# Mixture of experts, scatter back to the tokens: four experts' slot rows of one tile of tokens in 128 rows instead of two experts' rows of both tiles

## Chip, cores and metric

One core of one Trainium2 chip. The metric is the device time of one execution in microseconds (us), lower is better; the figure for a kernel is the median of its timed runs.

## What is computed

A trunk of two layers over 256 tokens (two tiles of 128) of width 1024. Each layer has a mixer of four head groups, a cross-attention into 256 memory tokens, and a grouped mixture of experts, each followed by a layer norm. The change touches the mixture of experts alone:

```python
# grouped_moe, cut
for e in range(N_EXPERTS):                                   # 16 experts
    h = jax.nn.silu(xt @ w_gate[e]) * (xt @ w_up[e])         # 1024 -> 256
    out = out + gates[:, e:e + 1] * (h @ w_down[e])          # 256 -> 1024
# gates: two experts per token, both inside the best of four groups; all others are 0
x = layer_norm(ALPHA * x + out, ln3_g[l], ln3_b[l])
```

## The kernel before, in words

Every token goes to two of the 16 experts, so the kernel doesn't multiply all tokens with all experts. It gives each expert 64 **slots**: 32 for tokens of tile 0 and 32 for tokens of tile 1 (a dense branch stands by for inputs that don't fit). The expert weights, 48 matrices of 1 MB per layer, stream from HBM through a ring of 12 buffers (`RING`, in the order of `expert_units`: gate and up matrices of pair j, then the down matrices of pair j-1). The sync engine's queue issues the loads in that order (`load`, L493; the DMA is issued on L512), and each waits until PE has finished with the matrix that lay in the buffer before.

The stage, per layer:

- DVE builds **one-hots** from each token's place (`one_hot`, L1531, the operation on L1534): per tile of tokens and half of the experts a 128x512 matrix, in which the columns of the other tile are zero. PE **gathers** token columns into slots with them (`part`, L2043, `gather_early`, `gather_late`), ACT and DVE move the result out of PSUM (`early_move`, `late_move`, L1572, L1580).
- PE brings each slot's gate value to its slot row (`gates_of_slots`, L2092, matmuls on L2096); DVE adds the high and low parts into `slot_gates` (L1612, L1617). PE transposes the one-hots (`to_token_turns`, L2100, transposes on L2105), ACT rounds the result into `to_token` (L967).
- For each **pair** j of experts (the two experts' 64 slots each fill 128 rows): `gate(j)`, `up(j)` (both L2122), the hidden values on ACT (`slots_tanh`, L923) and DVE (`hidden`, L1587, L1591), `turn(j)` (two transposes, L2144, moved by `turned_move`, L951), `down(j)` (16 matmuls in two halves of 512 columns, L2157).
- The output of `down(j)` is 128 slot rows by 1024 columns in PSUM. **Copies:** ACT rounds each half of 512 columns to `y_hi` (`out_high`, L953, operation on L958), DVE subtracts and leaves the rest in `y_lo` (`out_low`, L1594, operation on L1597). Two 128x512 operations on each engine per pair.
- **Scatter:** `scatter(j)` (L2163, matmuls on L2169) adds the pair's rows to the tokens' sum in the PSUM tensor `quad`: for each tile of tokens and each half of the columns one matmul with `y_hi` and one with `y_lo`, 8 matmuls of 512 columns a pair. Half of the 128 rows that each of them contracts over belong to slots of the other tile and are zero in `to_token`.

PE's order is written out at the end of its layer loop: the loop `for j in range(2, PAIRS)` runs gate(j), up(j), scatter(j-2), turn(j), down(j-1), and down(7) and the scatters of pairs 6 and 7 follow. DVE runs `hidden(j)`, then `out_low(j-1)`, and after the last `out_low` the third norm (`third_norm`, L1163): it adds `quad` to `X` (L1077) for tile 0 once `quad_ready` is set, then for tile 1 once `moe_done` is set. DVE takes its instructions in order, so the norm stands behind all copies.

Of the kernel before, what the change touches and what calls it, by code (L numbers as in the profile page):

```python
# [101 lines left out]
def hybrid_trunk_kernel(nc, x, mem, positions, w_in, gmlp_v_norm_g, gmlp_w_s, gmlp_b_s, mla_q_norm_g,  # L102
# [16 lines left out]
    PAIRS = E // 2  # L119
    MOE = expert_units(E)  # L120
# [53 lines left out]
    with ExitStack() as ctx:  # L174
# [60 lines left out]
        half_gates = sb("half_gates", [P, T, PAIRS, 4], F32R)  # L235
        before = sb("before", [P, P])
        slots = sb("slots", [P, T, EXPERT_SLOTS])
# [80 lines left out]
        to_token = rounded("to_token", 6000, PAIRS, SEQ)  # L318
# [11 lines left out]
        def to_slot(t):  # L330

            return (y_hi, y_lo)[t][:, 4:8, :].rearrange("p a b -> p (a b)")
# [20 lines left out]
        def y_of(y, j, a):  # L353

            return y[:, 4 * (j % 2) + 2 * a:4 * (j % 2) + 2 * a + 2, :]

# [208 lines left out]
        def _(pool):  # L565
# [13 lines left out]
            for t in range(T):  # L579
                nc.gpsimd.iota(slots[:, t, :], pattern=[[1, EXPERT_SLOTS]], base=-P - TILE_SLOTS * t,  # L580
                               channel_multiplier=0, allow_small_or_imprecise_dtypes=True)
# [93 lines left out]
        def _(act):  # L675
# [85 lines left out]
            for l in range(DEPTH):  # L761
# [165 lines left out]
                with act.If(act.value_load(fits[0:1, 0:1], min_val=0, max_val=1)):  # L927
# [38 lines left out]
                    for b in range(4):  # L966
# [13 lines left out]
                with act.Else():  # L980
# [13 lines left out]
                    act.sem_inc(out_hi, 2 * PAIRS)  # L994
# [4 lines left out]
        def _(dve):  # L999
# [182 lines left out]
            for l in range(DEPTH):  # L1182
# [348 lines left out]
                def one_hot(half, t):  # L1531

                    mine = place[:, t, E // 2 * half:E // 2 * (half + 1)]
                    nc.vector.tensor_tensor(to_slot(t)[:, 512 * half:512 * half + 512].rearrange("p (e s) -> p e s", e=E // 2),  # L1534
                                            view(slots[:, t, :], [[0, E // 2], [1, EXPERT_SLOTS]]),
                                            view(mine, [[1, E // 2], [0, EXPERT_SLOTS]]), ALU.is_equal).then_inc(slots_ready, 1)

                def all_gates():
# [5 lines left out]
                    of_pairs = gates[:].rearrange("p t (j e) -> p (t j) e", e=2)  # L1544
                    halves = half_gates[:].rearrange("p t j e -> p (t j) e")
                    nc.vector.tensor_scalar(halves[:, :, 0:2], of_pairs, 0.5, None, ALU.mult)
                    dve.drain()
                    nc.vector.scalar_tensor_tensor(halves[:, :, 2:4], of_pairs, 0.5, halves[:, :, 0:2].bitcast(F32),
# [762 lines left out]
```

## Time and profile before

| | |
|---|---|
| median of 3 runs | 722.87 us (722.40 to 724.38) |
| the profiled execution, its own time | 723.68 us |
| span of the profiled execution | 721.8 us |
| PE (matmul) busy | 697.4 us, 97% of the span |
| DVE busy | 408.0 us, 57% |
| ACT busy | 280.5 us, 39% |
| moved by DMA | 176.10 MB |

The profile is one execution. Times inside it count from the start of the span. PE is the matmul engine, DVE the vector engine, ACT the scalar engine. A timeline row gives start, duration, engine, line, operation, output and inputs, shape and how many instructions were merged; the brackets at its end hold the idle time before it and what ended that. Rows of one engine that follow each other closely can overlap by the depth of its pipeline, so the distance from start to start is the cost of one in a row. The stage of the experts stands in the trace from about 242 to 357 us (layer 1) and from about 594 to 709 us (layer 2).

### The profile page before, as it was taken

To read this page: it belongs to the slowest core of one execution; us is meant where nothing else is said; L and a number is where in the kernel's file an instruction comes from. 1 tells how busy PE (TensorE), PEld (TensorE's weight loads), DVE (VectorE), ACT (ScalarE), POOL (GpSimd) and SP (SyncE) were. 2 spreads that over 40 slices of the span, in tenths; PEclk is the share of its full clock that TensorE was granted. 3 is DMA by queue.
4 is the path that set the end of the run, shared out by engine and by line. 5 is a ranking of instruction groups with operands and counts; after the bars stand their busy time and mean duration, and the time that the engine had idled before them with its cause. 6 is when DMAs were issued, how large, how long until landed. Compare 5 with 4: busy or idle time off the path is not lost.

```text
span 721.8 us, 11939 instructions
## 1 busy us (share of the span) xinstructions
PE 697.4 (97%) x4744; PEld 560.4 (78%) x4744; DVE 408.0 (57%) x724; ACT 280.5 (39%) x471; POOL 48.3 (7%) x93
## 2 busy tenths in 40 slices
PE   7999999999999999999799999999999999999992
PEld 7989987889988875656399798888898897655551
DVE  4885886674575752111477588848646567212126
ACT  3545643355543331111424466435455252311111
POOL 1720000010041000000011000001000010000000
PEclk9999999999999999999989999999999999999997
DMA  8991334574358499999985313445633685999961
GB/s 283 332 366 57 113 126 171 186 238 153 118 189 343 191 382 400 414 417 414 359 298 168 127 59 118 157 164 194 239 124 110 239 349 222 355 420 417 415 269 61
DMA packets 62702, 176.10 MB, mean 244 GB/s; under 512 B 3872, under 2 KB 37104, under 8 KB 53424
## 3 DMA queue, kind: packets, MB, share of 16 engines
q1 hardware_dynamic: 58112, 161.69, 60.2%
q0 software_dynamic: 4096, 12.25, 5.1%
q10 hardware_dynamic: 432, 1.31, 0.5%
q8 instruction: 41, 0.67, 0.4%
q14 instruction: 21, 0.17, 0.1%
HBM read 174.19 MB, written 1.05 MB: 243 GB/s over the span
## 4 chain that ended last, share of the span: by engine, by line
PE 60%; issue 31%; DVE 3%; POOL 2%; DMA 1%; ACT 1%; DVEq 1%; POOLq 0%; ACTq 0%
PE ring L2122 8%; PE ring L1688 7%; PE ring L1689 7%; PE ring L1690 7%; PE ring L2157 4%; PE quad L1688 4%; PE quad L1689 4%; PE quad L1690 4%; PE quad L2169 2%; PE ring L1730 2%; PE ring L1856 1%; PE ring L1759 1%; DMA X<-in_x 1%; PE ring L1749 1%; PE ring L1954 1%
## 5 line engine op out<-in xcount | busy, mean ns | idle before, releaser
L1004 DVE TENSOR_TENSOR w_lo<-raw,w_hi 128x1024 fp32r<-128x1024 f32 x108 | 127.7, 1222 | 39.0 <-ACT w_hi L691 33.9
L691 ACT CAST w_hi<-raw 128x1024 fp32r<-128x1024 f32 x108 | 108.0, 1049 | 65.1 <-PE quad L1690 60.3
L1688 PE MATMUL ring<-x_hi,w_hi 128*128 128x256 f32 x320 | 92.9, 290 | 0.8 <-ACTq L734 0.7
L1689 PE MATMUL ring<-x_lo,w_hi 128*128 128x256 f32 x320 | 90.5, 283 | 0.0
L1690 PE MATMUL ring<-x_hi,w_lo 128*128 128x256 f32 x320 | 90.5, 283 | 0.0
L714 ACT ACTIVATE arena<-ring 128x512 f32<-128x512 f32 (+1 forms) x66 | 35.5, 573 | 84.7 <-PE ring L1690 65.1
L1597 DVE TENSOR_TENSOR y_lo<-ring,y_hi 128x512 fp32r<-128x512 f32 x32 | 22.1, 692 | 72.9 <-ACT y_hi L958 72.9
L1688 PEld LDWEIGHTS ring<-x_hi,w_hi 128*128 128x128 f32 x320 | 61.3, 192 | 2.3 <-issue 1.9
L1689 PEld LDWEIGHTS ring<-x_lo,w_hi 128*128 128x128 f32 x320 | 61.3, 192 | 0.7 <-issue 0.5
L1690 PEld LDWEIGHTS ring<-x_hi,w_lo 128*128 128x128 f32 x320 | 61.3, 192 | 0.0
L2122 PE MATMUL ring<-raw,x_slots 128*64 128x256 f32 x448 | 51.3, 380 | 0.0
L1688 PE MATMUL quad<-w_hi,y_hi 128*128 128x512 f32 x128 | 51.1, 399 | 0.0
L1689 PE MATMUL quad<-w_lo,y_hi 128*128 128x512 f32 x128 | 50.0, 391 | 0.0
L1690 PE MATMUL quad<-w_hi,y_lo 128*128 128x512 f32 x128 | 49.9, 390 | 0.0
L2122 PEld LDWEIGHTS ring<-raw,x_slots 128*64 128x64 f32 x448 | 32.0, 137 | 16.9 <-issue 1.1
L2122 PE MATMUL ring<-w_raw,x_slots 128*64 128x256 f32 x160 | 36.9, 380 | 0.0
L1688 PE MATMUL ring<-xb_hi,w_hi 128*128 128x256 f32 x128 | 36.5, 285 | 0.0
L2157 PE MATMUL ring<-w_raw,arena 128*64 128x512 f32 x144 | 36.1, 598 | 0.0
L1689 PE MATMUL ring<-xb_lo,w_hi 128*128 128x256 f32 x128 | 35.7, 279 | 0.0
L1690 PE MATMUL ring<-xb_hi,w_lo 128*128 128x256 f32 x128 | 35.7, 279 | 0.0
L1730 PE MATMUL ring<-ident 128*128 128x128 f32 x204 | 28.2, 301 | 6.9 <-issue 4.0
L958 ACT CAST y_hi<-ring 128x512 fp32r<-128x512 f32 x32 | 18.8, 586 | 41.4 <-PE ring L2157 41.4
(322 smaller groups left out, 1421.5 us busy)
## 6 DMA issues: line engine op xcount, KB each, us to landing
raw<-in_moe_w_gate SPq DMA_DIRECT2D x20, 1024.0 KB, 7.0
w_raw<-in_moe_w_down SPq DMA_DIRECT2D x18, 1024.0 KB, 10.9
raw<-in_moe_w_up SPq DMA_DIRECT2D x16, 1024.0 KB, 7.7
raw<-in_w_in SPq DMA_DIRECT2D x14, 1024.0 KB, 11.3
raw<-in_moe_w_down SPq DMA_DIRECT2D x12, 1024.0 KB, 10.1
raw<-in_w_out SPq DMA_DIRECT2D x10, 1024.0 KB, 5.1
raw<-in_xattn_wk SPq DMA_DIRECT2D x8, 1024.0 KB, 5.9
raw<-in_xattn_wv SPq DMA_DIRECT2D x8, 1024.0 KB, 4.8
```

The source lines that it names most:

```text
L691: nc.scalar.copy(unit_slot(u, 0, n)[:, s], raw[:, SLOT[u], s]).then_inc(hi_done, 1)
L714: nc.scalar.activation(dst, src, ACT.Copy, scale=scale).then_inc(act_emptied, 1)
L958: nc.scalar.copy(y_of(y_hi, j, a), out_bank(j, a).rearrange("p (a b) -> p a b", a=2)).then_inc(out_hi, 1)
L1004: low = nc.vector.tensor_tensor(unit_slot(u, 1, n)[:, s], raw[:, SLOT[u], s], unit_slot(u, 0, n)[:, s].bitcast(F32), ALU.subtract)
L1597: last = nc.vector.tensor_tensor(y_of(y_lo, j, a), out_bank(j, a).rearrange("p (a b) -> p a b", a=2), y_of(y_hi, j, a).bitcast(F32), ALU.s ...
L1688: mm(out, a_hi, b_hi, start=first, stop=False)
L1689: mm(out, a_hi, b_lo, start=False, stop=False)
L1690: return mm(out, a_lo, b_hi, start=False, stop=last)
L1730: mm(o[:, 0:P], ident[:], ident[:], start=True, stop=True)
L2122: r = mm(ring[of_pair(i), b, 0:FF], rows_of(2 * j + i, c), w[i][:, c, :], start=c == 0, stop=c == DC - 1)
L2157: r = mm(out_bank(j, a)[of_pair(i), :], h_t[:, j % 2, c * P:(c + 1) * P][:, of_pair(i)], w[i][:, c, 512 * a:512 * a + 512], start=c == 0, ...
L2169: r = mm(quad[:, 2 * t + a, :], to_token[:, j, t * P:(t + 1) * P], y_of(y, j, a).rearrange("p a b -> p (a b)"), start=j == 0 and i == 0, s ...
```

## The change

The slots stay (64 per expert, 32 per tile), and so do `gate`, `up`, `turn` and the matmuls of `down`. What changes is how the output rows are laid out for the scatter.

- `y_hi` and `y_lo` hold the rows of **four** experts (two pairs) for one tile of tokens: 4 x 32 = 128 rows. Each half of a pair's output is copied in four **quarters** of 32 rows by 512 columns, which start at another row in the output than in the input (`quarters`). So ACT and DVE each issue 8 operations of 32x512 a pair instead of 2 of 128x512, each with its own semaphore step.
- `scatter(k)` runs once for four experts: 8 matmuls of 512 columns for two pairs instead of 16. In the loop over pairs it stands at the odd j alone; at the even j `turn(j)` stands between the two halves of `down(j-1)`. After `down(7)` 8 matmuls follow instead of 16.
- The one-hots lose their zero columns: 128x256 instead of 128x512. There are 8 transposes instead of 16, 8 matmuls of 8 columns for the gates instead of 16 of 4, two moves to `to_token` instead of four.
- `slot_gates` is made by 8 reductions over 32 rows instead of two copies and two additions over 64 rows.

```diff
+        def quarters(j):
+            for t in range(T):
+                for i in range(2):
+                    q = 2 * (j % 2) + i
+                    yield t, slice(32 * q, 32 * q + 32), slice(64 * i + 32 * t, 64 * i + 32 * t + 32)
...
@@ ACT, out_high(j) @@
-                            nc.scalar.copy(y_of(y_hi, j, a),
-                                           out_bank(j, a).rearrange("p (a b) -> p a b", a=2)).then_inc(out_hi, 1)
+                            for t, to, rows in quarters(j):
+                                nc.scalar.copy(y_of(y_hi, t, a)[to],
+                                               out_bank(j, a)[rows].rearrange("p (a b) -> p a b", a=2)).then_inc(out_hi, 1)
...
-                    for b in range(4):
+                    for b in range(2):
                         last = nc.scalar.copy(to_token[:, 2 * b:2 * b + 2, :],
...
@@ DVE, out_low(j) @@
-                            dve.wait_ge(out_hi, l * 2 * PAIRS + (2 * j + a + 1))
-                            last = nc.vector.tensor_tensor(y_of(y_lo, j, a),
...
+                            for n, (t, to, rows) in enumerate(quarters(j)):
+                                dve.wait_ge(out_hi, l * 8 * PAIRS + (8 * j + 4 * a + n + 1))
+                                nc.vector.tensor_tensor(y_of(y_lo, t, a)[to],
+                                                        out_bank(j, a)[rows].rearrange("p (a b) -> p a b", a=2),
+                                                        y_of(y_hi, t, a)[to].bitcast(F32), ALU.subtract).then_inc(out_split, 1)
...
@@ DVE, slot_gates @@
-                    for e in range(2):
-                        rows = of_pair(e)
-                        parts = ring[rows, 3, 0:2 * E].rearrange("p (j e) -> p e j", e=4)
-                        nc.vector.tensor_copy(slot_gates[rows, :], parts[:, e, :])
...
+                    for j in range(2):
+                        for t, q, rows in quarters(j):
+                            parts = ring[q, 3, 0:4 * E].rearrange("p (k t h e) -> p k t h e", k=FOURS, t=T, h=2)
+                            nc.vector.tensor_reduce(slot_gates[rows, :].rearrange("p (k j) -> p k j", j=2)[:, :, j],
+                                                    parts[:, :, t, :, q.start // 32], AX_X, ALU.add)
...
@@ PE, gates_of_slots; to_token_turns changes in the same way @@
-                        for j in range(PAIRS):
+                        for k in range(FOURS):
                             for t in range(T):
-                                r = mm(ring[:, 3, 4 * j:4 * j + 4], to_slot(t)[:, j * P:(j + 1) * P],
-                                       half_gates[:, t, j, :], start=t == 0, stop=t == T - 1)
+                                at_col = 8 * (2 * k + t)
+                                r = mm(ring[:, 3, at_col:at_col + 8], to_slot(t)[:, k * P:(k + 1) * P], half_gates[:, t, k, :],
+                                       start=True, stop=True)
...
@@ PE, down(j, halves=range(2)): waits for out_split of the pair before, as it did @@
+                            if 0 < j < PAIRS - 1:
+                                pe.wait_ge(out_split, l * 8 * PAIRS + 8 * j)
...
-                    def scatter(j, tiles=range(T)):
+                    def scatter(k, tiles=range(T)):
 
                         for t in tiles:
                             for a in range(2):
-                                pe.wait_ge(out_split, l * 2 * PAIRS + (2 * j + a + 1))
+                                pe.wait_ge(out_split, l * 8 * PAIRS + (8 * (2 * k + 1) + 4 * a + 2 * (t + 1)))
                                 for i, y in enumerate((y_hi, y_lo)):
-                                    r = mm(quad[:, 2 * t + a, :], to_token[:, j, t * P:(t + 1) * P],
...
+                                    r = mm(quad[:, 2 * t + a, :], to_token[:, k, t * P:(t + 1) * P],
...
@@ PE, the order @@
                     for j in range(2, PAIRS):
                         gate(j)
                         up(j)
-                        scatter(j - 2)
-                        turn(j)
-                        down(j - 1)
+                        if j % 2:
+                            scatter(j // 2 - 1)
+                            turn(j)
+                            down(j - 1)
+                        else:
+                            down(j - 1, (0,))
+                            turn(j)
+                            down(j - 1, (1,))
                     down(PAIRS - 1)
-                    scatter(PAIRS - 2, (0,))
-                    scatter(PAIRS - 1, (0,)).then_inc(quad_ready, 1)
-                    scatter(PAIRS - 2, (1,))
-                    scatter(PAIRS - 1, (1,)).then_inc(moe_done, 1)
+                    scatter(FOURS - 1, (0,)).then_inc(quad_ready, 1)
+                    scatter(FOURS - 1, (1,)).then_inc(moe_done, 1)
```

## Rows read from the trace of the kernel before

**Rows 1.** The page: busy time of the engines, then data moved in 40 equal slices.
```profile
PE 697.4 (97%) x4744; PEld 560.4 (78%) x4744; DVE 408.0 (57%) x724; ACT 280.5 (39%) x471; POOL 48.3 (7%) x93
...
GB/s 283 332 366 57 113 126 171 186 238 153 118 189 343 191 382 400 414 417 414 359 298 168 127 59 118 157 164 194 239 124 110 239 349 222 355 420 417 415 269 61
```

**Rows 2.** Timeline of PE, one period of the pair loop, layer 1.
```profile
269.09 3.65 PE L2157 MATMUL ring<-w_raw,arena 128*64 128x512 f32 x16
...
276.03 3.62 PE L2122 MATMUL ring<-raw,x_slots 128*64 128x256 f32 x32
279.58 0.51 PE L2169 MATMUL quad<-y_hi,to_token 128*128 128x512 f32 x1
...
281.55 0.38 PE L2144 MATMUL ring<-ident,arena 128*128 128x128 f32 x2
281.86 3.65 PE L2157 MATMUL ring<-raw,arena 128*64 128x512 f32 x16
```

**Rows 3.** PE at the stage's head: a wait (us, times, longest us), then its timeline.
```profile
PEld ring L2045 <- DVE xn_lo L1455: 0.7, 2, 0.3
...
253.53 0.27 PE L2096 MATMUL ring<-half_gates,y_hi 128*128 128x4 f32 x1
...
255.34 0.37 PE L2045 MATMUL quad<-y_hi,xn_hi 128*128 128x256 f32 x1
...
261.03 0.33 PE L2105 MATMUL quad<-ident,y_hi 128*128 128x128 f32 x1
...
262.84 0.38 PE L2144 MATMUL ring<-ident,arena 128*128 128x128 f32 x2
```

**Rows 4.** Stretches: five engines, PE clock, DMA busy share, GB/s.
```profile
250.00:276.00 26.00, 26.00 (x214) 17.98 (x212) 13.12 (x21) 7.68 (x14) 0.00 (x0) 1.00 0.89 347
276.00:347.00 71.00, 71.00 (x500) 41.13 (x498) 12.32 (x22) 10.41 (x22) 0.00 (x0) 1.00 1.02 415
```

**Rows 5.** Two loads alone: duration ns, issue time, then time from issue to landing.
```profile
L512 SPq DMA_DIRECT2D w_raw<-in_moe_w_up x1: 367/367/367, 318.5 to 318.5; - x1
...
DMA to landing us min/median/max: 18.5/18.5/18.5
...
L512 SPq DMA_DIRECT2D arena<-in_moe_w_down x1: 414/414/414, 327.9 to 327.9; - x1
...
DMA to landing us min/median/max: 19.3/19.3/19.3
```

**Rows 6.** Timeline of PE, first use of those two loads, and down(6).
```profile
339.89 0.38 PE L2122 MATMUL ring<-mem_kT,arena 128*64 128x256 f32 x1
...
345.73 4.08 PE L2157 MATMUL ring<-w_raw,arena 128*64 128x512 f32 x17
349.22 0.59 PE L2157 MATMUL ring<-arena 128*64 128x512 f32 x1
```

**Rows 7.** Timeline of ACT and DVE: copies of pairs 6 and 7, then the third norm.
```profile
347.71 0.59 ACT L958 CAST y_hi<-ring 128x512 fp32r<-128x512 f32 x1 [1.50 <-PE ring L2157]
...
348.33 0.69 DVE L1597 TENSOR_TENSOR y_lo<-ring,y_hi 128x512 fp32r<-128x512 f32 x1 [4.22 <-ACT y_hi L958]
...
353.48 0.69 DVE L1597 TENSOR_TENSOR y_lo<-ring,y_hi 128x512 fp32r<-128x512 f32 x1 [1.03 <-ACT y_hi L958]
355.00 1.28 DVE L1077 SCALAR_TENSOR_TENSOR X<-X,quad 128x512 f32<-128x512 f32 x2 [0.83 <-PE quad L2169]
```

**Rows 8.** Timeline of DVE: operations that follow each other without a gap.
```profile
366.03 1.29 DVE L1029 TENSOR_TENSOR x_lo<-ring,x_hi 128x512 fp32r<-128x512 f32 x2
...
380.73 0.42 DVE L1232 COPY arena<-ring 128x256 f32<-128x256 f32 x1 [1.83 <-PE ring L1690]
381.17 0.42 DVE L1235 TENSOR_TENSOR arena<-ring,rope_cos 32x256 f32<-32x256 f32 x1
381.61 0.43 DVE L1236 TENSOR_TENSOR arena<-ring,rope_sin 32x256 f32<-32x256 f32 x1
...
256.63 0.34 DVE L1612 COPY slot_gates<-ring 64x8 f32<-64x8 f32 x2 [0.21 <-issue]
```

More of the change, by code:

```diff
@@ L119, in hybrid_trunk_kernel @@
     PAIRS = E // 2
+    FOURS = E // 4
     MOE = expert_units(E)
@@ L234, in hybrid_trunk_kernel @@
         gates = sb("gates", [P, T, E])
-        half_gates = sb("half_gates", [P, T, PAIRS, 4], F32R)
+        half_gates = sb("half_gates", [P, T, FOURS, 8], F32R)
         before = sb("before", [P, P])
-        slots = sb("slots", [P, T, EXPERT_SLOTS])
+        slots = sb("slots", [P, TILE_SLOTS])
         place = sb("place", [P, T, E])
@@ L317, in hybrid_trunk_kernel @@
         h_t = at(4608, 2, FF)
-        to_token = rounded("to_token", 6000, PAIRS, SEQ)
+        to_token = rounded("to_token", 6000, FOURS, SEQ)
         x_third = at(8048, DC, SEQ)
@@ L578, in _ @@
                                     pattern=[[1, P]], channel_multiplier=-1)
-            for t in range(T):
-                nc.gpsimd.iota(slots[:, t, :], pattern=[[1, EXPERT_SLOTS]], base=-P - TILE_SLOTS * t,
-                               channel_multiplier=0, allow_small_or_imprecise_dtypes=True)
+            nc.gpsimd.iota(slots[:], pattern=[[1, TILE_SLOTS]], base=-P, channel_multiplier=0,
+                           allow_small_or_imprecise_dtypes=True)
             pool.drain().then_inc(ident_ready, 1)
@@ L1608, in _ @@
                     dve.wait_ge(slot_gated, l + 1)
-                    for e in range(2):
-                        rows = of_pair(e)
-                        parts = ring[rows, 3, 0:2 * E].rearrange("p (j e) -> p e j", e=4)
-                        nc.vector.tensor_copy(slot_gates[rows, :], parts[:, e, :])
-                    dve.drain()
-                    for e in range(2):
-                        rows = of_pair(e)
-                        parts = ring[rows, 3, 0:2 * E].rearrange("p (j e) -> p e j", e=4)
-                        nc.vector.tensor_tensor(slot_gates[rows, :], parts[:, 2 + e, :], slot_gates[rows, :], ALU.add)
+                    for j in range(2):
[3 more added lines that the diff above has]
+                                                    parts[:, :, t, :, q.start // 32], AX_X, ALU.add)
                     dve.drain()
@@ L2043, in part @@
                 def part(half, c, t, x_part, first=False, last=False):
-                    one_hot = to_slot(t)[:, 512 * half:512 * half + 512]
-                    return mm(tile_slots(gather_bank(half, c), t), x_part[:, t, c, :], tile_slots(one_hot, t), start=first,
-                              stop=last)
+                    one_hot = to_slot(t)[:, SEQ * half:SEQ * half + SEQ].rearrange("p (e s) -> p e s", e=E // 2)
+                    return mm(tile_slots(gather_bank(half, c), t), x_part[:, t, c, :], one_hot, start=first, stop=last)
                 def gather_early():
@@ L2145, in turn, with down @@
                         r.then_inc(turned, 1)
-                    def down(j):
-                        pe.wait_ge(turned_moved, l * PAIRS + (j + 1))
-                        if 0 < j < PAIRS - 1:
-                            pe.wait_ge(out_split, l * 2 * PAIRS + 2 * j)
+                    def down(j, halves=range(2)):
+                        if 0 in halves:
+                            pe.wait_ge(turned_moved, l * PAIRS + (j + 1))
+                            if 0 < j < PAIRS - 1:
+                                pe.wait_ge(out_split, l * 8 * PAIRS + 8 * j)
                         w = [v.rearrange("p (c n) -> p c n", c=2)
                              for v in pair_wait((down_unit(2 * j), down_unit(2 * j + 1)))]
-                        for a in range(2):
+                        for a in halves:
                             for c in range(2):
```

39 lines of the change are left out of this document (17 added, 22 removed).

## Prediction

> **What bounds the kernel now.** I read the page first: PE is busy for 697.4 of 721.8 us, and in two stretches of the kernel the data moved stand at 414 to 420 GB/s for several slices in a row [rows 1]. Both are the stage of the experts. Two limits are near each other there, so I then read PE's timeline, the loads one by one, and the end of the stage.
>
> PE's timeline shows no gap in the pair loop. One period, from down to down, is 281.86 - 269.09 = 12.77 us; the scatter takes 281.55 - 279.58 = 1.97 us of it, and gate or up without one behind it is 3.45 us long, with one 3.55 us (from 276.03 to 279.58) [rows 2].
>
> The loads tell the other half. A period uses 6 matrices of 1.049 MB, which is 6.29 MB in 12.77 us or 493 GB/s. The transfers give 415 GB/s from 276 to 347 us with a busy share of 1.02, after 347 GB/s and 0.89 from 250 to 276 us [rows 4]. So PE eats faster than the transfers deliver, and lives on the 12 matrices that lay ready. The reserve is almost gone at the end: the second up matrix of pair 7 lands at 318.5 + 18.5 = 337.0 us, the last down matrix at 327.9 + 19.3 = 347.2 us [rows 5], and PE starts on them at 339.89 and 349.22 us [rows 6]. The slack is 2.9 and 2.0 us.
>
> The third thing to see is what ends the stage. down(6) starts at 345.73 [rows 6], the first copy on ACT 1.98 us later, DVE's first subtraction 2.60 us later (348.33), the last one at 353.48, and the norm's addition for tile 0 at 355.00 us [rows 7]. I measure the stage by that 355.00, since everything behind it keeps its order.
>
> **The change part by part** (layer 1; layer 2 repeats it, so all is doubled at the end).
>
> *Head.* 16 gate matmuls take 255.34 - 253.53 = 1.81 us, 16 transposes 262.84 - 261.03 = 1.81 us [rows 3]. Half of each goes: 0.9 + 0.9 us. The half-width one-hots shorten DVE: a 512-wide operation lasts 0.69 us [rows 7], a 256-wide one 0.42 us [rows 8], so the subtraction behind the first two comes up to 0.54 us earlier; PE waited for it 0.7 us in two times [rows 3], and gains 0.3 us. The second pair of one-hots, two moves to `to_token` and the iota end no wait: nothing. The 8 reductions for `slot_gates` replace 4 operations of about 0.17 us (two in 0.34 us, [rows 8]), so DVE needs some 0.7 us more; it has 0.5 us less to do before (the second pair of one-hots) and starts 0.3 us earlier, so nothing reaches PE. If that cover is gone, PE's wait ahead of the transposes is late by at most those 0.7 us. Head: 2.1 us earlier.
>
> *Pair loop.* The scatters at j = 2, 4 and 6 go. Each is 1.97 us, and mostly the 0.1 us at the change of shape stays with the turn: 2.0 us each, 6.0 us in all. PE could then start up(7) 8.1 us earlier, at 331.8 us. The copies there cost nothing: 8 operations of at most 0.8 us on DVE are 6.4 us, in a period that lasts over 10.7 us, and down(j) asks for them a full gate and up later.
>
> *But the weights.* In the stretch with share 1.02 a load lands when those before it have, not when it was issued. It gets earlier only as far as the whole queue starts earlier. The loads that fill the queue are issued when PE frees buffers at the head of the loop, and PE is there 2.1 us earlier. The bounds are 0 (nothing gained) and 26 us x (1 - 0.89) = 2.9 us (every idle bit between 250 and 276 us closed) [rows 4]. I take 2.1 us, what PE passes on. The last up matrix of pair 7 then lands at 334.9, the last down matrix at 345.1 us. Of 8.1 us gained, 3.1 us are waited away ahead of up(7): up(7) starts at 335.0, down(6) at 335.0 + 3.55 + 1.97 + 0.31 = 340.8 us, and down(7) at 345.2 us instead of 344.3 us.
>
> The Trainium skill ("DMA: Bandwidth & Descriptors", Where 436 GB/s comes from) names about 358 GB/s of HBM as the limit of a core and 435 GB/s as that of the fabric. This trace, with 415 GB/s from HBM, contradicts the lower figure; by it the waits would be longer still.
>
> *The copies at the end.* Now 16 quarters of pairs 6 and 7 stand on DVE in a row, where there were 4 wide ones. What one costs isn't in the trace, as no 32-row operation of 512 columns is there. Rows of parts of the partitions show that rows don't matter, columns do: 32x256 takes 0.42 us like 128x256. The distance from one to the next is bounded by two kinds of rows [rows 8]. Two operations over all 128 rows take 1.29 us for 0.69 us each, so the second starts after 0.60 us, inside the first. Those on another group of rows don't overlap with their neighbours, the 128-row one and the two 32-row ones behind it: 381.17 - 380.73 and 381.61 - 381.17 are 0.44 us each, for 0.42 us. The quarters change their group of rows every time, so they are nearest to the latter: 0.69 + 0.02 = 0.71 us. The same rows give the cost if each waits a little besides: 0.80 us, an estimate with 0.1 us on top of the duration.
>
> The Trainium skill ("VectorE: DVE Perf Modes", Two Vector instructions with no wait between them) says that an instruction that starts in another group of 32 partitions than the one before is held until that one has finished. The rows agree. Without that rule one would take 0.60 us from the wide rows; the result is the first rival.
>
> Sum: DVE's first quarter at 340.8 + 2.6 = 343.4 us; 16 x 0.71 = 11.4 us; the norm's addition 0.1 us later, at 354.9 us. ACT isn't the limit: at 0.59 us [rows 7] or less a quarter it stays ahead. The second chain, from the last load, ends no later: 345.2 + 2.6 + 8 x 0.71 = 353.5 us. The scatter of 8 matmuls fits between quarters, and tile 1 follows tile 0 on DVE.
>
> 354.9 against 355.00 is 0.1 us a layer, 0.2 us in all. The profiled execution took 723.68 us, 0.81 us over the median; taking the 0.2 us off the median of 722.87 gives 722.7 us. 24 scatter matmuls a layer go from the loop and 8 from the tail, and nearly all of it is eaten by transfers and copies.
>
> **The rivals.** The bound for "no change" is 0.3%, or 2.2 us (about what a measurement of this kernel can tell from it).
>
> *The quarters overlap on DVE* (0.60 us apart). For it: the wide rows. Against it: the narrow ones. 343.4 + 16 x 0.60 + 0.1 = 353.1 us, 1.9 us a layer, 3.8 us in all: 719.1 us. Chance 0.17.
>
> *The transfers don't hold PE.* For it: PE shows no wait for a load in the loop now. Against it: 493 wanted and 415 GB/s given, and slack of 2 to 3 us where 8 would be needed. down(6) at 345.73 - 8.1 = 337.6, the norm at 337.6 + 2.6 + 11.4 + 0.1 = 351.7 us: 3.3 us a layer, 716.3 us. Chance 0.10.
>
> *Slower: the loads land no earlier than before,* because the queue was nearly full from 250 us on. Place: the wait ahead of up(7). up(7) starts at 337.1, down(6) at 342.9, the norm at 357.0 us, 2.0 us a layer later: 726.9 us. It turns the result slower from a shift of the landings under 1.0 us (in place of 2.1). Against it is the 0.89. Chance 0.12.
>
> *Slower: the quarters cost 0.80 us.* 343.4 + 12.8 + 0.1 = 356.3 us, 1.3 us a layer: 725.5 us. It turns the result slower from 0.79 us a quarter on. Chance 0.06.
>
> **How the numbers follow.** The forecast has 0.55; of that 0.06 falls to faster (landings by the upper bound, 2.9 us earlier, and a bit of overlap) and 0.02 to slower, the rest within 2.2 us. Faster: 0.17 + 0.10 + 0.06 = 0.33. Slower: 0.12 + 0.06 + 0.02 = 0.20. Same: 0.55 - 0.06 - 0.02 = 0.47. The forecast's own range is 720.5 to 725.0 us. For 8 in 10 it must take in the first rival and the dearer quarters and may leave out most of the second and the worse half of the third: 717.5 to 726.0 us.
>
> **What would show it.** Right: PE idle ahead of gate(7), up(7) or down(7), ended by a load, some 3 to 4 us a layer; loads at about 415 GB/s and the last down matrix landing near 345 us; quarter subtractions 0.71 us from start to start in the tail, and the norm's first addition (L1077) within 1 us of 355.0; 64 scatter matmuls instead of 128, 1.81 us at the gates and the transposes halved. Wrong: no such wait (second rival), a distance of 0.60 us (first), landings near 347 us (third), DVE or ACT copies that PE waits for inside the loop, or a drop of PE's clock in the thinner tail that carries into the next layer.

## The result, and the profile after

The kernel after took 727.03 us (median; 725.61 to 729.63), the kernel before 722.87 us (722.40 to 724.38) beside it. The ratio is 1.0058, with a 95% interval of 1.0047 to 1.0068: slower by 4.2 us, outside the predicted range of 717.5 to 726.0 us and on its slow side. The profiled execution took 727.87 us, with a span of 726.0 us.

The first two fences are the page of the kernel after: busy times and groups of instructions (busy us and mean ns behind the bar), then the data moved. They answer to [rows 1]. A load **lands** when the last of its parts has arrived.

```profile
PE 683.7 (94%) x4648; PEld 548.4 (76%) x4648; DVE 473.0 (65%) x828; ACT 333.7 (46%) x563; POOL 48.2 (7%) x92
...
L1606 DVE TENSOR_TENSOR y_lo<-ring,y_hi 32x512 fp32r<-32x512 f32 x128 | 87.9, 687 | 51.1 <-ACT y_hi L966 47.5
...
L966 ACT CAST y_hi<-ring 32x512 fp32r<-32x512 f32 x128 | 73.9, 577 | 15.0 <-PE ring L2162 12.0
```

```profile
GB/s 282 331 362 71 106 140 168 187 242 126 129 208 343 204 380 402 417 416 410 318 276 175 117 59 117 171 164 188 232 116 116 232 348 246 371 418 417 417 216 60
```

PE lost 13.7 us of work and the span still grew by 4.2 us. DVE took 65 us more, for 104 instructions more. A quarter of 32 rows costs DVE 687 ns, as much as a wide copy of 128 rows. The transfers reach the same plateau for as many slices, at up to 418 GB/s (420 before).

The stretches show where PE's saving went; they answer to [rows 4] (five engines, granted clock of PE, busy share of the transfers, GB/s).

```profile
250.00:276.00 26.00, 25.96 (x216) 17.59 (x213) 17.28 (x31) 10.25 (x19) 0.00 (x0) 1.00 0.96 360
276.00:347.00 71.00, 66.09 (x466) 36.47 (x462) 33.72 (x53) 29.04 (x55) 0.00 (x0) 1.00 1.02 414
```

From 276 to 347 us PE was busy for all 71 us before and is now for 66.09 us, while the transfers go on as they did: 414 against 415 GB/s, share 1.02 both times. In the head the share rose from 0.89 to 0.96 and the rate from 347 to 360 GB/s.

What PE waits for stands in its timeline (layer 1); the third to fifth rows answer to [rows 6].

```profile
326.06 1.94 PE L2162 MATMUL ring<-raw,arena 128*64 128x512 f32 x8 [1.37 <-DMA raw<-in_moe_w_down]
...
331.04 1.95 PE L2126 MATMUL ring<-raw,arena 128*64 128x256 f32 x16 [0.80 <-DMA raw<-in_moe_w_gate]
...
337.25 0.40 PE L2126 MATMUL ring<-mem_kT,arena 128*64 128x256 f32 x1 [2.53 <-DMA w_raw<-in_moe_w_up]
...
343.14 3.65 PE L2162 MATMUL ring<-w_raw,arena 128*64 128x512 f32 x16
347.50 0.61 PE L2162 MATMUL ring<-w_raw,arena 128*64 128x512 f32 x1 [0.71 <-DMA arena<-in_moe_w_down]
```

The waits are 1.37 + 0.80 + 2.53 + 0.71 = 5.4 us; before there was none. The sum had 8.1 us of PE saved up to up(7). The first three waits took 4.7 us of that as the brackets count them, and down(6) starts 345.73 - 343.14 = 2.6 us earlier. The other 0.8 us lie in two places of PE's timeline. A period without a scatter, with the turn between the halves of down(j - 1), is 10.86 us long (gate to gate, 270.34 to 281.20), 1.9 us less than 12.77 and not 2.0: 0.3 us over three of them. The rest, 0.5 to 0.6 us, belongs to the waits: the last matmul ahead of a wait runs to its end with nothing behind it, and from start to start the three waits cost 5.3 us. The two loads behind the last two waits, alone, with issue time and time to landing; they answer to [rows 5]:

```profile
L520 SPq DMA_DIRECT2D w_raw<-in_moe_w_up x1: 2080/2080/2080, 313.5 to 313.5; - x1
...
L520 SPq DMA_DIRECT2D arena<-in_moe_w_down x1: 1671/1671/1671, 322.7 to 322.7; - x1
...
DMA to landing us min/median/max: 24.7/24.7/24.7
```

They are issued 5 us earlier than before (318.5 and 327.9) and land where they did: the up matrix at 337.1 us (before 337.0), the down matrix at 322.7 + 24.7 = 347.4 us (before 347.2).

The end of both layers is DVE's; the rows answer to [rows 7].

```profile
345.73 11.46 DVE L1606 TENSOR_TENSOR y_lo<-ring,y_hi 32x512 fp32r<-32x512 f32 x16 [4.22 <-ACT y_hi L966]
357.23 1.28 DVE L1085 SCALAR_TENSOR_TENSOR X<-X,quad 128x512 f32<-128x512 f32 x2
...
699.97 11.47 DVE L1606 TENSOR_TENSOR y_lo<-ring,y_hi 32x512 fp32r<-32x512 f32 x16 [4.22 <-ACT y_hi L966]
711.47 1.28 DVE L1085 SCALAR_TENSOR_TENSOR X<-X,quad 128x512 f32<-128x512 f32 x2
```

The sixteen quarters start 345.73 - 343.14 = 2.59 us behind down(6) and follow each other every (11.46 - 0.69) / 15 = 0.718 us. The norm's addition begins at 357.23 us, 2.2 us later than the 355.00 of before; in layer 2 at 711.47, 4.2 us later than the 707.30 of before. That is the whole loss.

### The profile page after: what moved, and what is told of

Same layout as the page of the kernel before. It is cut to its first block, busy times and chain, and to the rows that moved or that the text cites. A ratio compares the mean times of both kernels' runs of the same rounds, so it can differ in the third digit from the quotient of the medians.

```text
span 726.0 us, 11946 instructions
## 1 busy us (share of the span) xinstructions
PE 683.7 (94%) x4648; PEld 548.4 (76%) x4648; DVE 473.0 (65%) x828; ACT 333.7 (46%) x563; POOL 48.2 (7%) x92
## 4 chain that ended last, share of the span: by engine, by line
PE 53%; issue 32%; DVE 5%; DMA 4%; POOL 2%; ACT 2%; DVEq 1%; POOLq 0%; ACTq 0%; SPq 0%
PE ring L2126 6%; PE ring L1692 6%; PE ring L1694 6%; PE ring L1693 6%; PE quad L1692 4%; PE quad L1693 4%; PE quad L1694 4%; DMA w_raw<-in_moe_w_up 3%; PE ring L2162 2%; PE ring L1734 2%; PE ring L1860 1%; PE ring L1763 1%; PE ring L1958 1%; PE quad L2172 1%; DVE y_lo L1606 1%
## 5 line engine op out<-in xcount | busy, mean ns | idle before, releaser
L1606 DVE TENSOR_TENSOR y_lo<-ring,y_hi 32x512 fp32r<-32x512 f32 x128 | 87.9, 687 | 51.1 <-ACT y_hi L966 47.5
L966 ACT CAST y_hi<-ring 32x512 fp32r<-32x512 f32 x128 | 73.9, 577 | 15.0 <-PE ring L2162 12.0
L958 ACT COPY arena<-ring 128x256 f32<-128x256 f32 x16 | 6.0, 375 | 70.5 <-PE ring L2148 70.5
```

The costliest lines, as they stand in the source:

```text
L966: nc.scalar.copy(y_of(y_hi, t, a)[to], out_bank(j, a)[rows].rearrange("p (a b) -> p a b", a=2)).then_inc(out_hi, 1)
L1606: nc.vector.tensor_tensor(y_of(y_lo, t, a)[to], out_bank(j, a)[rows].rearrange("p (a b) -> p a b", a=2), y_of(y_hi, t, a)[to].bitcast(F32) ...
```

## The experiments

All times are medians, ratios are to the kernel before, run beside each kernel on the same chip (723.1 to 723.9 us there). Two kernels with another time for the kernel before beside them are best compared by their ratios. Diffs are against the kernel named.

**Theory:** the loads land at times fixed by the head of the stage, so PE's saved time is waited away, and what remains is a longer tail of copies. **Rivals:** PE's pace moves the landings; a quarter costs because of its rows or by holding PE; the thinner tail costs by PE's clock.

### Three scatters taken out of the kernel before

```diff
-                        scatter(j - 2)
+                        if j not in (3, 4, 6):
+                            scatter(j - 2)
```

> The kernel before, without the scatters at j = 3, 4 and 6 of the pair loop (pairs 1, 2 and 4 are left out of the sum). PE is free 6 us earlier ahead of up(7), nothing else changes; no copy is added. Loads limit the stage: the last up matrix of pair 7 lands near 337 us and the last down matrix near 347.2 us as before, PE waits for both, down(7) starts at about 347.3 us, the norm's first addition comes 5.8 us later at 353.1 us; 1.9 us a layer less than 355.0, so 3.8 us less in all (719.1 us). Rival, the loads follow PE and the copies alone made the changed kernel slower: all 6 us are kept, the norm at 349.0 us, 12 us less in all (711 us).

Measured: 722.23 us, ratio 0.9986 (0.9977 to 0.9996): far from both figures. The timelines of PE and DVE say why.

```profile
337.18 0.40 PE L2122 MATMUL ring<-mem_kT,arena 128*64 128x256 f32 x1 [1.30 <-DMA w_raw<-in_moe_w_up]
...
347.44 0.61 PE L2157 MATMUL ring<-w_raw,arena 128*64 128x512 f32 x1 [0.72 <-DMA arena<-in_moe_w_down]
```

```profile
353.26 1.29 DVE L1077 SCALAR_TENSOR_TENSOR X<-X,quad 128x512 f32<-128x512 f32 x2 [0.82 <-PE quad L2169]
```

```profile
358.62 2.93 PE L1730 MATMUL ring<-ident 128*128 128x128 f32 x12 [3.54 <-issue]
363.79 1.16 PE L1749 MATMUL ring<-ident,X 128*128 128x128 f32 x8 [2.23 <-issue]
```

Up to the norm it went as the theory has it. up(7) waits for its load and starts at 337.18, 0.07 us from the kernel after's 337.25, though both came there by different ways. The norm is 1.74 us earlier. Behind it PE stands still for 2.23 us ahead of the transposes of X with no releaser in the profile, though X had been ready since 361.34 us. That ate the gain of layer 1.

### The same number of instructions, narrow scatters

```diff
-                        scatter(j - 2)
+                        scatter(j - 2, width=64 if j in (3, 4, 6) else 512)
```

> The kernel before with three scatters (pairs 1, 2 and 4) of 64 columns in place of 512: as many instructions as before, 5 us less of PE a layer (the sums miss most of those pairs). In the first experiment the norm of layer 1 came 1.7 us early and PE then stood 2.2 us ahead of the transposes at 363.8 with no releaser in the profile, though X was ready at 361.3. Theory (the standstill came of where the shortened program's instructions were fetched): with the instructions as before it is gone, the transposes start at 361.8, and the time is 719.5 to 720.5 us. Rival (it came of the time at which PE gets there, or of the loads behind it): it is there again, 722 us.

Measured: 719.21 us, ratio 0.9938 (0.9921 to 0.9956). On DVE, then on PE:

```profile
352.97 1.28 DVE L1077 SCALAR_TENSOR_TENSOR X<-X,quad 128x512 f32<-128x512 f32 x2 [0.82 <-PE quad L2169]
```

```profile
358.83 2.50 PE L1730 MATMUL ring<-ident 128*128 128x128 f32 x12 [4.04 <-issue]
361.15 1.85 PE L1749 MATMUL ring<-ident,X 128*128 128x128 f32 x8
```

The norm begins 0.3 us from that of the first experiment, and the standstill is gone. The first experiment's kernel with lighter loads, described below, has as few instructions as the first, and its norm begins within 0.1 us of this run's (352.90 against 352.97). Its PE stands still again:

```profile
364.01 1.97 PE L1751 MATMUL ring<-ident,X 128*128 128x128 f32 x8 [2.29 <-DVEq L1117]
```

So the standstill goes with the number of PE's instructions, and not with when PE gets there. (The releaser named in that row, DVE's sign that X is ready, came at 360.98 us, 3 us before.) What causes it stays open. Instructions are fetched between 360 and 364 us, but in the narrow run and in the kernel before as well, with three packets of the same kinds.

A narrow scatter turned out to save 1.0 us and not 1.7 (DVE's copies come 1.0 us earlier behind each), so PE has 3 us less a layer here and 6 us less in the first experiment. Yet the norm is 2.0 us early in the one (355.00 to 352.97) and 1.7 us in the other: about 2 us a layer is all that is to be had from PE's work, and what goes beyond is waited away. In the first experiment that is 2.0 us ahead of up(7) and down(7), by the two waits above, and another 2.0 us for DVE ahead of three turns, which the scatters had covered.

### A later head

The first experiment's kernel, with the matmuls that spread the gates done twice:

```diff
-                        for j in range(PAIRS):
+                        for j in (*range(PAIRS), *range(PAIRS)):
```

> As the run without three scatters, but the 16 gate matmuls at the stage's head run twice, so PE frees the buffers of the head 1.8 us later. Loads pinned to their first issue (36 loads take 97 us from the first, whatever PE does later): landings, norm (353.1 us) and time (719.1 us) as in that run. Rival, landings shift with PE at the head, as the prediction had it: landings and norm 1.8 us later (354.9 us), 3.6 us more than that run (722.7 us).

Measured: 728.05 us, ratio 1.0052 (1.0034 to 1.0069). The extra matmuls cost more than I had counted, since the granted clock fell to half behind them (0.50 from 258 to 262 us, 0.87 as the mean of the head). The stretch, SP's next issue of loads, and the norm:

```profile
250.00:276.00 26.00, 26.00 (x192) 19.59 (x188) 11.64 (x18) 6.79 (x13) 0.00 (x0) 0.87 0.77 291
```

```profile
265.75 0.81 SPq L512 DMA_DIRECT2D raw<-in_moe_w_gate  x2
```

```profile
357.58 1.28 DVE L1077 SCALAR_TENSOR_TENSOR X<-X,quad 128x512 f32<-128x512 f32 x2 [0.83 <-PE quad L2169]
```

The third pair of refills was issued at 265.75 us, where the first experiment has it at 260.50 and the kernel before at 261.20. Now the transfers had a real hole (291 GB/s over the head, and 2 GB/s from 262 to 266 us). The last load landed at 330.0 + 21.6 = 351.6 us, 4.3 us later than without the extra matmuls; the norm is 357.58 - 353.26 = 4.3 us later too. Of the 5.25 us of delay in the head, 4.3 us came through to the last landing, and all of those to the norm. So neither figure stood (both were built on a smaller delay), but the landings do hang on the head, in the direction of later.

### Lighter loads

In three kernels here, and in a fourth at the end, the up matrices of experts 4 to 7 are loaded by an eighth:

```diff
+                if n0:
+                    dst, src = dst[:, 0:n0, :], src[:, 0:n0, :]
                 sp.dma_start(dst, src).then_inc(raw_full[SLOT[u]], 16)
...
-                    load(u, l, w[l, e].rearrange("(p c) n -> p c n", c=DC), (DC, FF))
+                    load(u, l, w[l, e].rearrange("(p c) n -> p c n", c=DC), (DC, FF), 1 if what == "u" and 4 <= e < 8 else None)
```

The kernel before:

> The kernel before with the up matrices of experts 4 to 7 loaded by an eighth only (their products are left wrong; about 3.6 MB less a layer). Theory: PE waits for no load in layer 1 of the kernel before, so nothing moves: 722.9 us. Rival (the transfers slow the kernel before as well, by their traffic or by the next stage's weights behind them): below 721 us.

Measured: 723.44 us, ratio 1.0006 (0.9996 to 1.0015). No change, as expected. But the last two landings moved by only 0.45 us here, so the run says little of what would follow if they moved by more.

The kernel after:

> The kernel after with the same lighter loads. Theory: the waits of PE for loads go, 5.4 us in layer 1 and 4.1 us in layer 2 of the kernel after's profile, so the copies of pairs 6 and 7 begin and end earlier by that: the norm of layer 1 at 351.8 instead of 357.2 us, 717.5 us in all. Rival (the quarter copies, not the loads, hold the kernel after along the whole loop): 725 us or more.

Measured: 723.51 us, ratio 1.0009 (0.9999 to 1.0018). That is 3.5 us off the kernel after's 727.03, a third of what I had written. PE and DVE, layer 1:

```profile
334.10 0.40 PE L2128 MATMUL ring<-mem_kT,arena 128*64 128x256 f32 x1 [1.46 <-DMA w_raw<-in_moe_w_up]
```

```profile
354.08 1.29 DVE L1087 SCALAR_TENSOR_TENSOR X<-X,quad 128x512 f32<-128x512 f32 x2
```

PE still waits for the loads: the lighter ones are early in the refill, and the later landings moved by only 3.1 us, which didn't end the waits. But up(7) moved by 3.15 us (337.25 to 334.10) and the norm by 3.15 us (357.23 to 354.08). The kernel after hangs on the landings one to one. In the kernel before PE's timeline shows no wait for a load in this stretch, in either version.

The kernel with fewer scatters:

> The kernel before without three scatters, as in the first experiment, and with the lighter loads. Theory: the waits of PE for loads that the first experiment's profile shows (2.0 us in layer 1, 1.5 us in layer 2) go too: 718.7 us, with the norm of layer 1 at 351.3 us. Rival (loads land no earlier because of PE's own pace, and nothing hangs on them): 722.2 us as without the lighter loads.

Measured: 721.81 us, ratio 0.9981 (0.9972 to 0.9991), against 722.23 us without the lighter loads. There the last landing moved by 0.4 us only, and the norm with it by 0.4 us (352.90). The figure was wrong, as lighter loads early in the refill needn't bring later ones forward; by itself this run tells the two theories apart weakly.

### Wide subtractions, four times

The kernel before, where DVE does each wide subtraction of pairs 6 and 7 four times, all over the same 128 rows:

```diff
+                            if j >= 6:
+                                for n in range(3):
+                                    spare = at(512 * (3 * a + n), 512)
+                                    nc.vector.tensor_tensor(spare, out_bank(j, a), y_of(y_hi, j, a), ALU.subtract)
```

> The kernel before; ACT copies as before, but DVE does each 128x512 subtraction of pairs 6 and 7 once for real and three more times into spare memory, so 16 of them stand in a row as in the run with quarters, all on the same group of rows. If a change of the group of rows makes the quarters dear: start to start 0.60 us here against 0.72 us there, the norm at 358.0 us (3.0 us a layer, 6 us in all, 728.9 us). Rival, the distance comes from something else that both have (a read of PSUM in a row): 0.72 us here too, the norm at 359.9 us, 732.7 us.

Measured: 729.20 us, ratio 1.0077 (1.0061 to 1.0094).

```profile
347.93 1.88 DVE L1604 TENSOR_TENSOR arena<-ring,y_hi 128x512 f32<-128x512 f32 x3
```

```profile
357.06 1.27 DVE L1077 SCALAR_TENSOR_TENSOR X<-X,quad 128x512 f32<-128x512 f32 x2
```

On the same rows a copy follows the one before after (1.88 - 0.69) / 2 = 0.60 us; the quarters, which change rows, after 0.718 us. The sixteen quarters pay 16 x 0.12 = 1.9 us a layer for that. The real subtractions among the wide ones wait for ACT and set a semaphore as the quarters do, and where ACT had long been done they too follow after 0.60 us (354.67 against 354.07 for the last of the three before it), so the semaphores aren't the price. No run has operations of 32 rows that stay on the same rows, so the row count and the change of rows are told apart only by the rows of before, where a narrow operation lasts as long as a wide one [rows 8]. The Trainium skill ("VectorE: DVE Perf Modes", Two Vector instructions with no wait between them) has the second instruction held until the first has finished when it starts in another group of 32 partitions; both distances agree with it.

### Quarters in the kernel before

Only the copies of pairs 6 and 7 cut into quarters, with the scatters left alone:

```diff
+                            for q in range(4) if j >= 6 else (None,):
+                                rows = slice(0, P) if q is None else slice(32 * q, 32 * q + 32)
...
-                            nc.scalar.copy(y_of(y_hi, j, a),
-                                           out_bank(j, a).rearrange("p (a b) -> p a b", a=2)).then_inc(out_hi, 1)
+                                nc.scalar.copy(y_of(y_hi, j, a)[rows],
+                                               out_bank(j, a)[rows].rearrange("p (a b) -> p a b", a=2)).then_inc(out_hi, 1)
```

> The kernel before, with the copies of pairs 6 and 7 alone cut in quarters of 32 rows (same rows in and out), the sum unchanged. Quarters held at 0.72 us each on DVE: first one at 348.3 us, 16 x 0.72 later the norm, at 359.9 us instead of 355.0, 4.9 us a layer, 9.8 us in all (732.7 us). Rival, quarters that overlap at 0.60 us: the norm at 358.1 us, 3.1 us a layer, 6.2 us in all (729.1 us); the rest of the changed kernel's loss would then lie elsewhere.

Measured: 737.92 us, ratio 1.0198 (1.0181 to 1.0215), 5 us over the dearer of the two. DVE, then PE:

```profile
347.93 11.45 DVE L1602 TENSOR_TENSOR y_lo<-ring,y_hi 32x512 fp32r<-32x512 f32 x16 [4.21 <-ACT y_hi L960]
360.70 1.28 DVE L1079 SCALAR_TENSOR_TENSOR X<-X,quad 128x512 f32<-128x512 f32 x2 [1.31 <-PE quad L2173]
363.90 1.29 DVE L1079 SCALAR_TENSOR_TENSOR X<-X,quad 128x512 f32<-128x512 f32 x2 [1.92 <-PE quad L2173]
```

```profile
359.44 0.80 PE L2173 MATMUL quad<-y_hi,to_token 128*128 128x512 f32 x1 [1.72 <-DVE y_lo L1602]
...
361.31 0.63 PE L2173 MATMUL quad<-y_hi,to_token 128*128 128x512 f32 x1
```

The chain of quarters is as long as in the kernel after (11.45 us), so the change's price of the tail is there alone. What comes on top is that here every scatter matmul needs all four quarters of a half, so ten of them stand behind the last copy, and at half the clock (0.63 us each, 0.43 from start to start, against 0.40 and 0.23 at the full one). In the kernel after only two matmuls stand behind the last quarters, since its quarters come in the order "tile 0 first".

### The scatters of the kernel after, twice

```diff
                             scatter(j // 2 - 1)
+                            scatter(j // 2 - 1, again=True)
```

> The kernel after with each of the three scatters in its loop done twice (24 matmuls of some 0.24 us, 6 us of PE a layer, as much as the change took out; the pairs 0 to 5 are added twice). Theory: PE waits 5.4 us for loads in layer 1 of the kernel after, so the extra 6 us fill those waits: down(6) starts 0.6 us later than at 343.1, the time is 727 to 728.5 us. Rival (PE's own work sets the pace and the saved scatters had been worth their time): 12 us more, 739 us.

Measured: 730.66 us, ratio 1.0103 (1.0085 to 1.0121).

```profile
336.56 0.40 PE L2126 MATMUL ring<-mem_kT,arena 128*64 128x256 f32 x1 [0.96 <-DMA w_raw<-in_moe_w_up]
```

```profile
346.92 11.46 DVE L1606 TENSOR_TENSOR y_lo<-ring,y_hi 32x512 fp32r<-32x512 f32 x16 [6.10 <-ACT y_hi L966]
```

12 us more of PE cost 3.6 us by the medians (3.3 us by the ratios), so the rival's 12 are out. It is more than the 0 to 1.5 us that I gave. A part of it has a reason that I had overlooked: the last of the three stands between up(7) and down(6), behind PE's last wait ahead of the copies, and costs its 1.9 us in full. up(7) came 0.7 us earlier, as its load did, so the copies start 1.9 - 0.7 = 1.2 us later (346.92 against 345.73). The other two vanish in the waits of layer 1. In layer 2 the norm is another 0.6 us late. That makes 1.8 us, which is the distance of the two profiled executions (729.74 against 727.87 us); what the medians have beyond it isn't in them.

### Fours in the loop, wide copies at the end

The kernel after, with pairs 6 and 7 scattered as before; their one-hots (padded with zeros) are turned in the head as well.

```diff
+                            if j >= PAIRS - 2:
+                                nc.scalar.copy(y_wide(y_hi, j, a),
+                                               out_bank(j, a).rearrange("p (a b) -> p a b", a=2)).then_inc(out_hi, 1)
+                                continue
                             for t, to, rows in quarters(j):
...
-                    scatter(FOURS - 1, (0,)).then_inc(quad_ready, 1)
-                    scatter(FOURS - 1, (1,)).then_inc(moe_done, 1)
+                    scatter_wide(PAIRS - 2, (0,))
+                    scatter_wide(PAIRS - 1, (0,)).then_inc(quad_ready, 1)
+                    scatter_wide(PAIRS - 2, (1,))
+                    scatter_wide(PAIRS - 1, (1,)).then_inc(moe_done, 1)
```

> Pairs 0 to 5 are scattered by fours, pairs 6 and 7 as before, with wide copies; the head turns four one-hots more. Theory (the loads' landings are fixed by when the refill begins, so PE's saved scatters are waited away, and what the change loses is the tail of sixteen copies): the loads' last landings stay near 337.1 and 347.3 us, down(6) starts near 343.1, and the norm of layer 1 starts near 353.3 us as in the run with fewer scatters, against 357.2 in the kernel after: 722.5 us in all. Rival (the copies by quarters in the loop cost too, by holding PE or by delaying slots of the weights): the norm stays at 355 or later and the time is 725 us or more.

Measured: 717.53 us, ratio 0.9932 (0.9918 to 0.9946): faster than both kernels, and by 5 us better than I had written.

```profile
345.96 0.61 PE L2191 MATMUL ring<-w_raw,arena 128*64 128x512 f32 x1 [1.07 <-DMA arena<-in_moe_w_down]
```

```profile
351.78 1.29 DVE L1101 SCALAR_TENSOR_TENSOR X<-X,quad 128x512 f32<-128x512 f32 x2 [0.82 <-PE quad L2212]
...
703.01 1.28 DVE L1101 SCALAR_TENSOR_TENSOR X<-X,quad 128x512 f32<-128x512 f32 x2 [0.82 <-PE quad L2212]
```

The norm is 5.45 us earlier than in the kernel after in layer 1, 8.46 us in layer 2. The tail gives 3.9 us in layer 1, the landings the other 1.5 us. The 5 us that I missed can be placed in part. The profiled execution took 719.36 us, 2.4 us less than that of the first experiment (721.80), whose time I had taken as the basis. The standstill of 2.2 us isn't here, and the last load of layer 1 landed at 345.82 us where I had 347.3. Against that, the loads of layer 2 landed 1.0 us later, counted from layer 1's norm (697.06 - 351.78 against 697.25 - 352.97 in the narrow run). The median of 717.53 lies another 1.8 us below the execution that was profiled, and no trace shows why.

The same kernel with the lighter loads:

> The kernel with fours for pairs 0 to 5 and wide copies for 6 and 7, its up matrices of experts 4 to 7 loaded by an eighth only. Theory: in the wide-tailed kernels the norm of layer 1 starts 5.96 us after the last load has landed (347.30 to 353.26 and 345.82 to 351.78 us), so whatever the lighter loads move that landing by, the norm moves by: if by 1.5 to 3 us as in the kernel after, 713 to 716 us in all. Rival (PE's waits for the turn and the copies hold this kernel once its tail is wide): the norm stays at 351.8, 717.5 us in all.

Measured: 716.67 us, ratio 0.9900 (0.9883 to 0.9917). Here the lighter loads moved the last landing of layer 1 the other way, by 0.5 us, and the norm went with it (352.33 us); in layer 2 both came 2.1 us earlier (the norm at 700.87). The profiled executions are 2.2 us apart (719.36 and 717.12), the ratios 2.3 us. The time followed the landings, though the landings didn't follow the lighter loads as I had thought.

### What the runs have in common

Landing times from the completion records of the loads (us; U: second up matrix of pair 7, D: last down matrix), and the start of the norm's first addition, N:

```
kernel                       layer 1                     layer 2
                         U       D       N           U       D       N
before                 336.96  347.22  355.00      689.20  699.34  707.30
lighter loads, before  336.50  346.77  354.75      688.75  698.89  707.05
after                  337.11  347.37  357.23      691.35  701.52  711.47
lighter loads, after   333.97  344.23  354.08      686.77  696.96  706.89
fewer scatters         337.05  347.30  353.26      689.31  699.45  705.41
narrow scatters        336.75  347.01  352.97      687.10  697.25  703.22
fours, then wide       335.22  345.82  351.78      686.95  697.06  703.01
same, lighter loads    336.10  346.36  352.33      684.77  694.91  700.87
```

In the two kernels with the quarter tail N is U + 20.11 or 20.12 us, in both layers. In the four with less PE work and the wide tail N is D + 5.95 to 5.97 us, in both layers. The first experiment with lighter loads and the one with the late head, which aren't in the table, keep it too (D + 5.96 to 5.97 us). The kernel before keeps neither distance (D + 7.8 and 8.0 us): its end was PE's. That is the theory in numbers that repeat to 0.02 us. The kernel after with its scatters done twice has U + 22.0 us in layer 1, the 20.1 us and the 1.9 us of the scatter behind up(7).

## Why the prediction was wrong

**The head** was right: gates, transposes and first subtraction bring PE 2.2 us earlier to down(0) (266.86 against 269.09), where 2.1 were forecast.

**The loop** was right: 2.2 + 3 x 1.9 = 7.9 us of PE's work up to up(7) are gone, where the sum had 8.1, PE waits for loads, and the copies in the loop hold nobody.

**"But the weights"** is the step that failed. I let the landings come 2.1 us earlier ("I take 2.1 us, what PE passes on"), between bounds of 0 and 2.9 us. They came 0.15 us later than before, at 337.11 and 347.37 us where the forecast had 334.9 and 345.1. It was the lower bound that held, and with it the third rival, nearly to the digit: up(7) at 337.25 (337.1 there), down(6) at 343.14 (342.9), the norm at 357.23 (357.0), 727.03 us in all (726.9).

Why PE's lead isn't passed on shows in the completion records. Each load has 16 of them, one for each DMA engine that carries a part. For the tenth load to land from 250 us on, the first of the 16 was done at 279.9 us and the last at 280.78 us in the kernel before; in the kernel after the first at 278.3 us and the last at 280.78 us. Most of the earlier issue did reach the faster engines, and the load landed when it had, with the slowest. The next five loads land within 0.02 us of each other in the two kernels. Then each slips once by about 1 us: the kernel before at the sixteenth load, the kernel after only at the up matrix of pair 7. In the head the rate went from 347 to 360 GB/s, which is 0.34 MB or 0.8 us at 415 GB/s: I had read the share of 0.89 as idle time that an earlier issue would fill, but it is a mean over 16 engines, and by these records the one that counted had less of it. A later issue is another matter: in the experiment with the late head 4.3 of 5.25 us of delay came through.

The digits of the rival owe something to luck. For sixteen loads, from 295.83 to 333.39 us, the kernel after was 0.9 to 1.1 us ahead, and the slip at the very load that up(7) waits for took that away. Had it come one load later, up(7) would have started some 1.2 us earlier, an estimate from the size of the slip. Layer 2 shows the same end without a slip so late: counted from layer 1's norm, U lands after 334.20 us before and 334.12 us after.

The slips have a companion in the traces. Instructions are fetched in packets of 16 KB, which take about 1.1 us. One began at 293.15 us in the kernel before, one at 334.49 us in the kernel after, each at the load that slipped. At U in the kernel after the fifteenth of the 16 parts was done at 335.88 us and the last alone at 337.11. In layer 1, from 280 to 348 us, the thirteen traces have ten landings that come 0.7 us or more later than the usual 2.5 us behind the one before, and each has such a packet, begun at most 0.8 us before the earlier landing and before the later one; of all the intervals there fewer than one in five has one. Not every packet makes a slip (the one of 310.11 us in the kernel after made none). No run moved the fetches by themselves, so this is a companion and not a shown cause. In layer 2 it is looser: from 640 us on four of six slips have one.

What sets the landing to a microsecond stays open beyond that. Among the kernels with full loads whose first refill was issued between 249.2 and 250.3 us, and whose head wasn't lengthened, the last landing of layer 1 varies from 345.82 (fours, then wide) to 347.37 us.

**The copies** were right in price: 0.718 us each against 0.71. The rule on the row groups held, and the rivals of 0.60 and 0.80 us are out. But I had their chain begin at 343.4 us, and it began at 345.73; I had written the sum as two changes that cancel. The earlier landings didn't come, and the longer chain was paid.

**PE's clock** in the thinner tail, named among what could go wrong, didn't matter. Of the kernel after:

```profile
355.00:360.00 5.00, 2.67 (x6) 1.37 (x6) 4.66 (x8) 3.00 (x5) 0.00 (x0) 0.62 1.09 350
360.00:365.00 5.00, 1.65 (x7) 1.65 (x8) 4.14 (x7) 2.78 (x5) 2.74 (x5) 0.50 0.46 127
```

```profile
382.71 0.42 DVE L1240 COPY arena<-ring 128x256 f32<-128x256 f32 x1
```

The kernel before was granted 1.00 and 0.51 in these two stretches. But DVE was the one to wait for, and the 2.2 us by which the norm is late are 2.0 us at this copy, which stood at 380.73 [rows 8].

**The chances.** The rival with fixed landings got 0.12, against the single number 0.89. Nothing else in the profile of before spoke for the 2.1 us: the stretch behind had the share 1.02 and the landings every 2.5 us, which says that a queue is full, not how early it got so.

## What to carry to other kernels

Where a stage is fed by a full queue, find the landing that the end of the stage hangs on and write the end as that landing plus a tail; work saved ahead of the landing is worth nothing beyond the slack that was there, work added behind it costs in full. A change that trades one for the other should be split: here the half in the loop, kept with the old tail, gives 717.5 us where the whole gives 727.0. A busy share below one, as a mean over 16 engines, needn't be room for an earlier issue, as one of them may have none.

## What the runs showed of the hardware that I had not expected

- A load lands with the slowest of its 16 engines, and these drift apart: from 280 us to the end of the stage in layer 1 the spread from first to last completion is 0.9 to 2.1 us in the kernel before and 2.4 to 3.8 us in the kernel after.
- A landing that slips by 0.7 us or more in a full queue had an instruction packet of 16 KB beside it in ten of ten cases of layer 1 (four of six in layer 2). The cause isn't shown by a run of its own.
- A standstill of PE of 2.2 to 2.3 us, with nothing in the profile that explains it, came in two kernels with 24 matmuls a layer fewer and was gone with the same 24 at an eighth of the columns, with the norm ahead of it at the same time within 0.1 us for one of the two. It was gone too when 16 small matmuls a layer were added in the head. In the first experiment and the narrow one the transposes behind it started at 363.79 and at 361.15 us, which is most of the 3.0 us between those two kernels.
- 3 us less of PE's work a layer brought layer 1's norm 2.0 us forward, 6 us less 1.7 us. The bound is the last landing plus 5.96 us.
